# One modulation chunk multiplied ahead of attention instead of inside it, in a two-layer transformer kernel

## The reference, cut to what matters

```python
mod = cond @ p['w_mod'] + p['b_mod']                  # (1024) @ (1024, 6*1024)
sh1, sc1, g1, sh2, sc2, g2 = jnp.split(mod[:, None, :], N_MOD, axis=-1)
h = rms_norm(x, p['g_pre_mix']) * (1.0 + sc1) + sh1
y, k, v = mixer(h, p, l, ctx_kv, ang)                 # conformer, Hyena, differential attention
x = x + g1 * rms_norm(y, p['g_post_mix'])
h = rms_norm(x, p['g_pre_ffn']) * (1.0 + sc2) + sh2
y = moe(h.reshape(B * L, D), p).reshape(B, L, D)
x = x + g2 * rms_norm(y, p['g_post_ffn'])
```

## Time and profile before

| | |
|---|---|
| median of 3 runs (lowest to highest) | 1689.54 us (1686.64 to 1689.78) |
| profiled execution | 1686.68 us, span 1684.8 us, mean granted PE clock 0.984 |
| PE busy | 1559.6 us (93%) |
| DVE, ACT, POOL busy | 866.6, 362.0, 469.1 us |
| chain that ended last | PE 65%, DMA 25%, DVE 5%, ACT 2% |
| chunk loads (2 MB each) | median 11.8 us from issue to landing in RING, 10.8 us in KSYS |

### The profile page before, as it was taken

The page is one execution under the profiler, slowest core; times in us unless marked ns, Lnnn a source line. Parts: engine busy times, 40 slices in busy tenths (PEclk is TensorE's granted clock), DMA queues, the critical chain, the costliest instruction groups (busy, mean ns, idle before and its releaser), DMA issues.

```text
span 1684.8 us, 23039 instructions
## 1 busy us (share of the span) xinstructions
PE 1559.6 (93%) x7996; PEld 802.8 (48%) x7996; DVE 866.6 (51%) x2815; ACT 362.0 (21%) x792; POOL 469.1 (28%) x437
## 2 busy tenths in 40 slices
PE   6999899899998999999979997998999989999996
PEld 2886355444444444444447853563444444444443
DVE  3789653644444444434266987455444344444432
ACT  2521443111111111111153224440111111111111
POOL 0350010233333233333114301004333333233320
PEclk9999999999999999999989999999999999999998
DMA  9422915799999999999732248039999999999993
GB/s 399 155 102 105 380 84 200 288 410 413 413 413 416 413 412 414 412 415 412 299 131 100 101 161 357 1 110 398 388 412 414 413 415 412 413 413 413 415 413 164
DMA packets 80853, 530.62 MB, mean 315 GB/s; under 512 B 13968, under 2 KB 17308, under 8 KB 25184
## 3 DMA queue, kind: packets, MB, share of 16 engines
q1 hardware_dynamic: 67680, 503.90, 73.7%
q0 software_dynamic: 13056, 25.22, 4.0%
HBM read 533.76 MB, written 5.77 MB: 320 GB/s over the span
## 4 chain that ended last, share of the span: by engine, by line
PE 65%; DMA 25%; DVE 5%; ACT 2%; issue 2%; SPq 1%; POOL 0%; DVEq 0%; ACTq 0%
PE PSB L978 24%; DMA RING<-in_exp_w_up 13%; DMA WB<-in_exp_w_up 9%; PE PSB L991 8%; PE PSB L885 4%; PE PSB L1025 3%; PE PSB L1026 3%; PE PSB L970 2%; DMA RING<-in_wmod 2%; PE PSB L702 2%; PE PSB L921 1%; PE PSB L948 1%; PE PSB L931 1%; PE PSB L922 1%; PE PSB L947 1%
## 5 line engine op out<-in xcount | busy, mean ns | idle before, releaser
L978 PE MATMUL PSB<-RING,EX 128*32 128x512 f32 (+2 forms) x1408 | 373.3, 606 | 27.3 <-DMA RING<-in_exp_w_up 14.1
L978 PE MATMUL PSB<-WB,EX 128*32 128x512 f32 (+2 forms) x1344 | 371.5, 598 | 22.9 <-DMA WB<-in_exp_w_up 13.0
L576 POOL DMA_INDIRECT XG<-h_rows,IDX x272 | 279.8, 1029 | 146.5 <-issue 72.8
L585 POOL TENSOR_SCALAR SCAT<-CST,LSTT 128x384 fp32r<-128x384 f32 x68 | 85.6, 1259 | 560.8 <-DVE IDX L1863 519.1
L991 PE MATMUL PSB<-RING,AT 128*32 128x512 f32 (+2 forms) x752 | 210.8, 597 | 0.0
L978 PEld LDWEIGHTS PSB<-RING,EX 128*32 128x32 f32 (+2 forms) x1408 | 115.9, 126 | 182.0 <-issue 182.0
L978 PEld LDWEIGHTS PSB<-WB,EX 128*32 128x32 f32 (+2 forms) x1344 | 114.4, 127 | 177.4 <-issue 177.4
L1939 DVE TENSOR_TENSOR YL<-PSB,YH 128x512 fp32r<-128x512 f32 x136 | 94.1, 692 | 188.9 <-ACT YH L1431 188.9
L991 PE MATMUL PSB<-WB,AT 128*32 128x512 f32 (+2 forms) x672 | 189.1, 597 | 0.0
L1855 DVE COPY LCOL<-PSB 128x6 f32<-128x6 f32 x68 | 11.2, 165 | 338.8 <-PE PSB L1009 293.9
L1025 PE MATMUL PSB<-YH,SCAT 128*128 128x512 f32 x408 | 171.7, 421 | 2.8 <-DVE YL L1939 2.8
(11 more groups left out here) (299 smaller groups left out, 2005.8 us busy)
## 6 DMA issues: line engine op xcount, KB each, us to landing
RING<-in_exp_w_gate SPq DMA_DIRECT2D x64, 1024.0 KB, 14.5
RING<-in_exp_w_up SPq DMA_DIRECT2D x64, 1024.0 KB, 18.0
WB<-in_exp_w_gate SPq DMA_DIRECT2D x64, 1024.0 KB, 14.7
WB<-in_exp_w_up SPq DMA_DIRECT2D x64, 1024.0 KB, 19.0
RING<-in_exp_w_down SPq DMA_DIRECT2D x64, 1024.0 KB, 18.4
WB<-in_exp_w_down SPq DMA_DIRECT2D x64, 1024.0 KB, 19.0
RING<-in_wmod SPq DMA_DIRECT2D x16, 2048.0 KB, 11.8
KSYS<-in_wmod SPq DMA_DIRECT2D x8, 2048.0 KB, 10.8
```

The costliest lines, as they stand in the source:

```text
L576: pool.indirect_dma_start(XG[:, s % 2, g * 256:(g + 1) * 256], None, h_quarters, bass.IndirectOffsetOnAxis(ap=IDX[:, s, g:g + 1], axis=0), ...
L585: nc.gpsimd.tensor_scalar(SCAT[:, s % 2, :], cst("iota"), LSTT[:, s:s + 1], None, ALU.is_equal).then_inc(p_scat, 1)
L978: mm = nc.tensor.matmul(PS[6][s0:s0 + w, :].rearrange("p (w f) -> p w f", w=2), e(k, s0, w), rawgu[n % NBUF][:, k], start=(k == 0), stop=( ...
```

## The change

The first of attention's eight chunks is multiplied ahead of tile 17, right behind the query turns, in both layers. Units 0 to 6 then take the second to the eighth chunk, and `mod_columns` moves from unit 8 to unit 7. Since banks 6 and 7 now hold the chunk's sums while keys are still to be turned, the turns move to banks 3 and 4. These are tile 16's and tile 18's, so the first turn gains a wait for tile 16's copy by ACT (`a_u`), and tile 18 gains a wait for the seventh turn's copies (`a_qk`). SP loads the fourth chunk, whose slot comes free with the first, ahead of the second and the third.

```diff
--- before.py
+++ after.py
@@ -374,8 +374,11 @@
 
         def fill(l, i):
 
-            first = 4 if l == 0 else 16
-            return first + i if i < 8 else None, 2 * l + 1 if i == 8 else None
+            return early(l) + 1 + i if i < 7 else None, 2 * l + 1 if i == 7 else None
+
+        def early(l):
+
+            return 4 if l == 0 else 16
 
         def pieces(l, i):
 
@@ -485,14 +488,15 @@
                 tiles_done(l, 10)
                 weight_in(l, "t2")
                 tiles_done(l, 13)
-                mod_in(fill(l, 0)[0])
+                mod_in(early(l))
                 tiles_done(l, 16)
                 sp.dma_start(KT[:, :, P:2 * P], I["ck"][l]).then_inc(ctx_in, 16)
                 weight_in(l, "o0")
+                mod_in(early(l) + 3)
                 sp.wait_ge(pe_conv, 4 * (l + 1))
-                mod_in(fill(l, 1)[0])
+                mod_in(early(l) + 1)
                 tiles_done(l, 19)
-                mod_in(fill(l, 2)[0])
+                mod_in(early(l) + 2)
                 for c, out in ((1, "ok"), (2, "ov")):
                     sp.wait_ge(a_u, K_AU * l + au(10 + 3 * c))
                     sp.dma_start(O[out][0, l].rearrange("h s d -> s h d"),
@@ -820,10 +824,12 @@
                 n = NH * c + h
                 if h == 0:
                     pe.wait_ge(d_rope, K_ROPE * l + 12 * (c + 1))
+                if n == 0:
+                    pe.wait_ge(a_u, K_AU * l + au(16))
                 if n >= 2:
                     pe.wait_ge(a_qk, 12 * l + (n - 1 if n < 6 else 4 + 2 * (n - 5)))
                 for t in range(NT):
-                    mm = nc.tensor.transpose(PS[6 + n % 2][:, t * P:(t + 1) * P],
+                    mm = nc.tensor.transpose(PS[3 + n % 2][:, t * P:(t + 1) * P],
                                              QKV[:, t, 512 * c + h * P:512 * c + (h + 1) * P], ident)
                 mm.then_inc(pe_qk, 1)
 
@@ -1236,10 +1242,12 @@
                 z_spectra(l, 1)
                 for h in range(NH):
                     qk_turn(l, 0, h)
+                mod_chunk(early(l))
                 u_tile(l, 17)
                 z_conv(l, 1)
                 for h in range(NH):
                     qk_turn(l, 1, h)
+                pe.wait_ge(a_qk, 12 * l + 10)
                 u_tile(l, 18)
 
                 pe.wait_ge(a_qk, 12 * (l + 1))
@@ -1522,10 +1530,10 @@
                 n = NH * c + h
                 act.wait_ge(pe_qk, 8 * l + n + 1)
                 if c == 0:
-                    own.sig(sc.activation(QT[:, h, :], PS[6 + n % 2][:, 0:TOK], ACT.Copy), a_qk)
+                    own.sig(sc.activation(QT[:, h, :], PS[3 + n % 2][:, 0:TOK], ACT.Copy), a_qk)
                 else:
-                    own.sig(sc.activation(KT[:, h, 0:P], PS[6 + n % 2][:, 0:P], ACT.Copy), a_qk)
-                    own.sig(sc.activation(KT[:, h, 2 * P:4 * P], PS[6 + n % 2][:, P:TOK], ACT.Copy), a_qk)
+                    own.sig(sc.activation(KT[:, h, 0:P], PS[3 + n % 2][:, 0:P], ACT.Copy), a_qk)
+                    own.sig(sc.activation(KT[:, h, 2 * P:4 * P], PS[3 + n % 2][:, P:TOK], ACT.Copy), a_qk)
 
             for l in range(DEPTH):
                 act.wait_ge(par_in, 16 * (l + 1))
```

## The result

The changed kernel took 1695.20 us (median of 20 runs, 1690.76 to 1703.86), the kernel before 1687.94 us beside it. The ratio is **1.0038, 95% interval 1.0028 to 1.0048**: 6.4 us slower (4.7 to 8.1). The forecast was 4.2 us. One run of the kernel before, of 8413.93 us, is in no ratio.

What follows compares the result with a forecast made beforehand. Attention was taken as bound by the load queue behind the third chunk's issue, most clearly in layer 1. Shifts of 2.2 + 1.3 us made +3.5, with one clock fall +4.2; added to 1689.54 that gave 1693.7 us, range 1688.6 to 1698.0.

Steps and rivals of the forecast that it cites:

- T: Issue of the third chunk's load in each layer, where the load queue starts; forecast 2.16 us later per layer.
- The early chunk: First chunk multiplied ahead of tile 17: eight matmuls, 1.85 us, so tile 18 ends that much later.
- The wait of tile 18: Tile 18 waits for the seventh turn's copies, forecast 0.3 us (0.31 in the sum) per layer.
- From unit 3 on the landings stand where they stood, counted from T: Units 3 to 5 still take the queue's second to fourth loads; unit 6 2.2 us later in layer 1, 1.3 in layer 0.
- the queue's fourth load hold unit 5: Layer 0: unit 5's chunk there at 198.55 instead of used at 197.02; unit 6's row maximum 1.3 us later.
- The wait at unit 1: Unit 1 now wants the queue's first load: a new PE wait of 3.0 to 3.2 us in both layers.
- That sign: Sign to look for in the trace: unit 3's chunk starts 15.7 to 16 us after T, as before.
- one fall of two: Clock drop after unit 1's wait, 0.9 us in layer 0 and 0.5 in layer 1; one taken, giving +4.2 us.
- The sum with both: Both layers' shifts, +3.5 us at full clock, with a clock fall in both layers: +4.9 us.
- Carried unchanged to the layer's end: Shift at unit 6 taken through to the layer's end unchanged, as everything up to the first expert load is one chain.
- The likeliest case: The forecast's own case, +4.2 us, 46%; range 1690.9 to 1697.0 for later clock stretches, up to 1.2 us per layer.
- third rival: Slower by more: clock falls at unit 1 in both layers and one more each at unit 8, +7.3 us, 1696.8; 15%.

Runs made afterwards that it cites:

- the run with the banks alone: Changed kernel with the first chunk back in unit 0 and loads in their old order, keeping the turns' new banks and waits: 1689.05 us, 1.0001 to the kernel before.
- The delay alone: Kernel before with nine useless multiplications of constants ahead of tile 17, nothing else changed: 1692.37 us, 1.0019 to the kernel before.
- the late fourth load: Changed kernel with the fourth chunk's load put back behind the third and the cache outputs: 1702.96 us, 1.0078 to the kernel before.
- PE kept busy: Changed kernel with eleven multiplications of constants ahead of unit 1's chunk, so PE works while it loads: 1691.27 us, 1.0016 to the kernel before.

## Why the prediction was right, and where its sizes were off

**T moves by 2.16 us per layer: 2.51 measured.** The early chunk cost 1.95 us between the second group of query turns and tile 17 (153.17 to 155.88 for 149.79 to 150.55) and another 0.10 in tile 17, where 1.85 was put down: a tile behind a chunk took 6.97 us to the next start instead of 6.87. The wait of tile 18 cost 0.46 us (0.48 in the run with the banks alone) for 0.31 forecast: 0.36 ahead of the tile, and again 0.10 in it. Both terms were short, by some 0.10 for the tile that follows and 0.05 to 0.10 in front of it.

**From unit 3 on the landings stand where they stood, counted from T: right for units 4 to 6 of layer 1**, and this decided the sign. Their chunks start within 0.02 us of their old places from T (unit 5's at 25.59 for 25.61) and unit 6's scores at 28.42 for 28.43; unit 6's row maximum was forecast at 29.5 us from T and measured at 29.46. That is closer than the mechanism alone gives: the chain of waits there is DVE's from unit 4's scores on, which came 18.96 us after T for 18.04, and the loads held PE for only 0.58 and 0.16 us at units 4 and 5, so that two paths happened to end together. In layer 0 the forecast had the queue's fourth load hold unit 5; there PE waited for no load behind unit 1, but 1.43 us for DVE, as before the change. The delay alone and the late fourth load show the rule from two sides: places kept within 0.9 us, and places one load later.

**The wait at unit 1 (3.0 to 3.2 us): there in both layers, smaller** (2.72 and 2.08): the queue's first load was there 8.80 and 8.17 us after T, and the terms had taken 9.0 to 9.2 over from the kernel before. Unit 3's chunk was not gated by its load at all: it started 16.6 us (layer 1) and 17.1 us (layer 0) after T, where 15.7 to 16 was foretold, because PE came late from unit 1 at half clock. That sign did not come; in layer 1 it cost nothing, as the short waits at units 4 and 5 took it up.

**The clock: one fall of two was taken, both came.** The sum with both was +4.9 us, and unit 6's scores are 2.18 us later in layer 0 (2.52 up to T, less 0.34 from T) and 2.46 in layer 1 (2.47 less 0.01): 4.64 us. That the two agree is in part luck. T moved 0.35 us more per layer than forecast, while the falls at unit 1 cost next to nothing by unit 6, where 0.9 and 0.5 us were put down for them: with PE kept busy both were gone, and unit 6's scores came 28.55 and 28.36 us after T for 28.74 and 28.42. The rule cited from the Trainium skill's page TensorE: Matmul & The Clock Gate, section HAM oscillation, held at unit 1 in both layers, though the waits in the page's own case, some 3 to 5 us, are longer than the 2.72 and 2.08 us here. It is no certainty: of 20 waits of 1.5 to 3.1 us ahead of a chunk, in the attention of the thirteen profiles, 17 were followed by a chunk that took 2.60 to 3.64 us, and three, of 1.52, 2.06 and 2.59 us, by one of 1.92.

**Carried unchanged to the layer's end: wrong in layer 0.** The kernel before had a stretch at half clock behind unit 9's scores (four rows of the output weight took 3.01 us at 219.55, 1.88 at full clock). The changed kernel ran that part at full clock; its own such stretch came earlier, at 213.59, where PE waited for DVE on both sides of it, and 1.4 us were back by the gate's turns (244.49 for 240.37, less 3.38 of the start, is 0.74 us late). Then four rows of the shared expert's weight ran at half clock (3.22 us at 294.96, 1.96 before) and the 1.5 us were gone again at the first expert load. Before, then after:

```profile
219.55 3.01 PE L885 MATMUL PSB<-RING,YT 128*128 128x512 f32 x4
...
240.37 1.95 PE L835 MATMUL PSB<-CST,GC 128*128 128x128 f32 x16
```

```profile
213.59 3.39 PE L687 MATMUL PSB<-FOLD,CO 128*128 128x8 f32 x16
...
244.49 1.95 PE L841 MATMUL PSB<-CST,GC 128*128 128x128 f32 x16
...
294.96 3.22 PE L984 MATMUL PSB<-RING,HT 128*128 128x512 f32 x4
```

Such stretches come and go without the change meaning them: from the gate's turns to the first expert load six of the thirteen profiles take 68.55 to 68.59 us and seven 67.03 to 67.06, and kernels with and without the early chunk are among both. The likeliest case's own range was drawn for them.

**The size in all.** The two profiles show +4.7 us as the change's (8.1 less the 3.38 of the start), against +4.2 forecast; it would be 3.2 us without the 1.5 us of the stretch just named. The runs say 6.4, with 4.7 at the edge of the interval, and so lie nearer to the third rival's +7.3 than to 4.2. Of that rival's falls those at unit 1 are there, and unit 8's scores ran at half clock in both layers (1.65 us at 218.60 and 1050.49); but from T to the gate's turns the changed kernel is 1.8 us shorter and 0.1 longer, so the profile shows no price for them. What makes up the rest stays open: no run shows how often the late start and the stretch ahead of the first expert load came among the twenty runs. The run with PE kept busy, 3.7 us better though its attention is no shorter, points to more falls of the clock in the changed kernel; it doesn't prove it. The time itself, 1693.7 us forecast and 1695.20 measured, came nearer than the difference only because the kernel before stood at 1687.94 us beside it, 1.6 us under the 1689.54 that the forecast started from.

## What to carry to other kernels

When loads queue behind one moment, ask of every unit which place in the queue it wants, not how many loads there are: multiplying one chunk ahead of the queue helped nobody, since every unit then wanted one place further, while leaving one unit without a load moved all behind it up and was worth 7 us here. Work that is moved ahead of the instruction which releases a buffer delays everything that buffer feeds, here by its own size and a little more. And where a load is put one unit later, read the queue's order once more: a load behind another that waits for a slot waits too.

## What was not expected

Two cache outputs in the middle of the load queue cost the kernel before 4.9 us (2.2 to 7.6), where without them the fourth chunk starts only 1.5 us sooner after T in layer 0 (14.34 for 15.86) and 2.3 in layer 1 (13.37 for 15.65); in layer 0 the longer wait was followed by a fall of the clock, the shorter was not. And the start of the kernel, before any of this, is some 3.4 us longer in two profiles of thirteen.
